# Sixty-four columns of ones in place of one in a kernel's column sums

## The reference, cut to what matters

```
def rms_norm(x, g):
    xf = x.astype(jnp.float32)
    y = xf * lax.rsqrt(jnp.mean(xf * xf, axis=-1, keepdims=True) + EPS)
    return (y * g.astype(jnp.float32)).astype(x.dtype)

def l2_norm(x):
    xf = x.astype(jnp.float32)
    return (xf * lax.rsqrt(jnp.sum(xf * xf, axis=-1, keepdims=True) + EPS)).astype(x.dtype)
...
    q = jnp.repeat(l2_norm(q), rep, axis=2) * DN_HEAD_DIM ** -0.5      # delta rule: 12 heads
    k = jnp.repeat(l2_norm(k), rep, axis=2)                            # 12 heads
...
    o = rms_norm(o.astype(p.dtype), out_g)                             # 24 heads of the mixer's output
...
    q = rms_norm(xq.reshape(B, S, XA_HEADS, XA_DIM), qn_g)             # cross-attention: 4 heads
    k = rms_norm(kv[..., :XA_WIDTH].reshape(B, -1, XA_HEADS, XA_DIM), kn_g)
```

## Time and profile before

| | us |
|---|---|
| median of 3 runs | 3015.46 |
| lowest and highest run | 3014.51, 3021.64 |
| profiled execution, its own time | 3011.83 |
| its span, first to last instruction | 3010.0 |
| PE busy / PEld busy | 2836.4 (94%) / 2672.0 (89%) |
| DVE busy / ACT busy / POOL busy | 1903.9 (63%) / 1411.2 (47%) / 386.0 (13%) |
| TensorE's mean granted clock | 0.973 of full speed |

### The profile page before, as it was taken

How to read it: one execution, slowest core, us unless ns; L and a number is a source line. 1 busy time by engine, 2 the same in 40 slices (tenths; PEclk the granted TensorE clock), 3 DMA queues, 4 the chain that set the end, 5 groups by cost and what they waited for, 6 DMA issues and landing times.

```text
span 3010.0 us, 46274 instructions
## 1 busy us (share of the span) xinstructions
PE 2836.4 (94%) x19298; PEld 2672.0 (89%) x19298; DVE 1903.9 (63%) x2814; ACT 1411.2 (47%) x2387; POOL 386.0 (13%) x360
## 2 busy tenths in 40 slices
PE   6999989889889999999989999998999999999997
PEld 6999989888888998999979999997888899987785
DVE  5546648533323544655456865776888888878786
ACT  5346543555654433444344204343555555555454
POOL 0000010211111000003100002221122211112320
PEclk9999989999999999999999999999999999999998
DMA  4443444422223554444434458998999988899894
GB/s 185 169 154 140 169 131 167 154 77 94 85 94 112 198 186 166 167 169 162 154 114 169 156 204 322 374 357 312 366 361 371 366 319 322 321 350 349 319 350 147
DMA packets 109680, 668.46 MB, mean 222 GB/s; under 512 B 25777, under 2 KB 26313, under 8 KB 31553
## 3 DMA queue, kind: packets, MB, share of 16 engines
q1 hardware_dynamic: 83808, 496.08, 45.2%
q0 software_dynamic: 24512, 164.97, 15.0%
q10 hardware_dynamic: 1152, 4.47, 0.4%
HBM read 651.54 MB, written 13.30 MB: 221 GB/s over the span
## 4 chain that ended last, share of the span: by engine, by line
PE 72%; DVE 12%; DMA 8%; ACT 7%; issue 2%; POOL 0%; SPq 0%; DVEq 0%; ACTq 0%
PE PS L1027 71%; DMA raw<-in_pv 4%; DVE WL L1641 4%; DVE m L1632 3%; DMA m<-in_pv,keep 3%; ACT m L2322 2%; ACT WH L2337 2%; ACT L2322 1%; DVE m L1841 1%; DVE m L2162 1%; DMA raw<-in_w_kv 1%; DVE m L1838 0%; PE PS L1030 0%; ACT m L2323 0%; DVE m L1660 0%
## 5 line engine op out<-in xcount | busy, mean ns | idle before, releaser
L1641 DVE TENSOR_TENSOR WL<-raw,WH 128x1024 fp32r<-128x1024 f32 x804 | 985.5, 1234 | 650.6 <-ACT WH L2337 649.6
L2337 ACT CAST WH<-raw 128x1024 fp32r<-128x1024 f32 x804 | 837.5, 1046 | 551.5 <-PE PS L1027 390.2
L1027 PE MATMUL PS<-m_4096r,WH 128*128 128x256 f32 x5184 | 997.3, 293 | 29.9 <-DVE m L1632 14.7
L1027 PEld LDWEIGHTS PS<-m_4096r,WH 128*128 128x128 f32 x5184 | 827.8, 196 | 53.2 <-DVE m L1632 16.1
L1027 PE MATMUL PS<-m_4096r,WL 128*128 128x256 f32 x2592 | 743.6, 287 | 0.0
L1027 PE MATMUL PS<-m_8192r,WH 128*128 128x256 f32 (+1 forms) x2560 | 559.7, 312 | 17.5 <-issue 11.1
L1027 PE MATMUL PS<-WH,m_896r 128*128 128x512 f32 x1536 | 523.1, 393 | 28.2 <-DVE m_896r L2255 27.9
L1027 PEld LDWEIGHTS PS<-m_4096r,WL 128*128 128x128 f32 x2592 | 507.6, 196 | 0.0
L1027 PEld LDWEIGHTS PS<-m_8192r,WH 128*128 128x128 f32 x2560 | 397.6, 193 | 20.3 <-issue 11.7
L1027 PE MATMUL PS<-m_8192r,WL 128*128 128x192 f32 (+1 forms) x1792 | 404.3, 272 | 0.0
L1027 PE MATMUL PS<-WL,m_896r 128*128 128x512 f32 x1024 | 400.8, 391 | 0.0
(11 more groups left out here) (234 smaller groups left out, 1857.7 us busy)
## 6 DMA issues: line engine op xcount, KB each, us to landing
raw<-in_pu SPq DMA_DIRECT2D x128, 1024.0 KB, 6.8
raw<-in_pv SPq DMA_DIRECT2D x128, 1024.0 KB, 8.0
raw<-in_w_qkv SPq DMA_DIRECT2D x48, 1024.0 KB, 4.8
raw<-in_w_o SPq DMA_DIRECT2D x48, 1024.0 KB, 4.8
raw<-in_w SPq DMA_DIRECT2D x40, 1024.0 KB, 4.8
raw<-in_w_z SPq DMA_DIRECT2D x32, 1024.0 KB, 4.8
raw<-in_w_kv SPq DMA_DIRECT2D x16, 1024.0 KB, 4.8
raw<-in_w_q SPq DMA_DIRECT2D x16, 1024.0 KB, 4.8
```

What stands on the lines that cost most here:

```text
L1027: return e.matmul(o, l, x, start=start, stop=stop)
L1641: tt(WL[:, k, :], raw[:, n % NRAW, h * 1024:h * 1024 + 1024], WH[:, k, :].bitcast(F), ALU.subtract).then_inc(S["lo"], 1)
L2337: e.copy(WH[:, k, :], raw[:, n % NRAW, h * 1024:h * 1024 + 1024]).then_inc(S["hi"], 1)
```

## The change

Every column sum now takes the first 64 columns of the tile of ones, so each gives 64 equal columns. The first of them stands where the one column stood; the other 63 stand to its right. Sums are issued in rising order of their column, so the next sum writes over what the last left to the right of its own column, and the columns that are read hold what they held before. In `hn_sum` the two matmuls of one sum write the same 64 columns, the second adding. Up to column 70 (`hn_sum`), 110 (`rn_sum`) and 66 (`dn_yss`) of the bank is written in place of 7, 47 and 3. No instruction is added or removed, no wait, no transfer and no order is changed.

```
+            def add_up(bank, c, x, start=True, stop=True):
+
+                return mm(PS[:, bank, c:c + 64], x, C("ones")[:, 0:64], start, stop)
...
-                            m = mm(PS[:, 2, 2 * h + t:2 * h + t + 1], tile(SQ, 2 * h + i)[:, tok(t)], C("ones")[:, 0:1],
-                                   i == 0, i == 1)
+                            m = add_up(2, 2 * h + t, tile(SQ, 2 * h + i)[:, tok(t)], i == 0, i == 1)
...
-                    m = mm(PS[:, 2, 2 * i + t:2 * i + t + 1], x[:, tok(t)], C("ones")[:, 0:1], True, True)
+                    m = add_up(2, 2 * i + t, x[:, tok(t)])
...
-                    m = mm(PS[:, bA, i:i + 1], blk(dn(g, "kb"), i), C("ones")[:, 0:1], True, True)
+                    m = add_up(bA, i, blk(dn(g, "kb"), i))
```

## The result

| | before | after |
|---|---|---|
| median, lowest to highest | 3018.38 us, 3014.51 to 3021.64 (5 runs) | 2995.59 us, 2993.34 to 3002.26 (5 runs) |
| profiled execution, its own time | 3011.83 us | 2993.34 us |
| its span | 3010.0 us | 2991.5 us |
| mean granted clock | 0.973 | 0.978 |

The ratio is 0.9929 with a 95% interval of 0.9914 to 0.9944: the change makes the kernel faster, as forecast, by 22.8 us between the medians. The forecast was a gain of 12.0 us, to 3003.5 us, with a range from 2998 to 3012. The measured time lies 2.4 us under the range. The two profiled executions lie 18.5 us apart.

What follows compares the result with a forecast made beforehand. TensorE was taken to bound the kernel on most of the way. 12.4 us back from the clock less 0.4 us latency gives 12.0 us off 3015.5, so 3003.5 us; range 2998 to 3012, chance 0.60.

Steps and rivals of the forecast that it cites:

- That the wider passes cost nothing: On TensorE, the 256 column-sum passes: 64 columns hide behind the next pass's weight load, 0 us; at most 13.6 us.
- That the clock holds in the padded blocks: TensorE's granted clock stays at 1.00 throughout all six `hn_sum` and `rn_sum` blocks, where 27.30 us had been at 0.50.
- The comparison with wide passes and pauses: From 29.48 to 36.30 us, 256-column passes kept 1.00 with TensorE busy 3.65 of 6.82 us; the padded block moves more.
- Rival B: No change (3015.9 us): the clock falls in the padded blocks too, only the latency of 0.4 us is paid; chance 0.10.
- The 12.4 us from the low stretches: Five half-clock stretches at `hn_sum` and `rn_sum`: 4.0 us back from column sums, 8.4 us from mostly weight passes.
- That the shift reaches the end unchanged: Behind 401.61 us ACT and DVE begin earlier by the same amount, so the whole gain reaches the end.
- Latency, 0.4 us: At 15 group ends ACT waits some 25 ns longer for the last matmul: 0.4 us added, between 0 and 0.8.
- `dn_yss`, 0: Padding these sums might save the low stretch at 940.84 us, 1.5 us; taken as 0 because the pause stays.
- A: Only part arrives (3009.5 us): where low stretches begin is chance, the changed kernel may fall elsewhere; 6 us back; chance 0.17.
- D: More (3000 us): timed runs lose 3.6 us more to the same stretches, or the 940.84 us stretch goes; chance 0.10.
- The Trainium skill's rule read as busy time: The clock follows how busy TensorE is, so the drops at busy one-column blocks have another cause and padding gives nothing.
- the last one of the sum: Whole kernel: the 12.0 us gain is taken from the three timed runs' median, 3015.5 us, giving 3003.5 us.

Runs made afterwards that it cites:

- second profile: The kernel before, unchanged, profiled and timed again in a later job: 3001.74 us median, ratio to the kernel before 0.998.
- fourfold sums: Every matmul of `rn_sum` issued four times over, against the kernel before: 3062.11 us with one column, 3036.99 us with 64 columns in `rn_sum` only.
- first and third: The kernel before, unchanged: profiled execution of 3011.83 us at first, and profiled and timed again in a later job, 3008.99 us, ratio 1.0005.

## Why the prediction was right and wrong

- **That the wider passes cost nothing**: right. 0.108 to 0.110 us a pass with 64 columns, against the 0.109 and 0.106 of the rows on either side; 128 columns cost nothing either.
- **That the clock holds in the padded blocks**: right in all four profiles of the changed kernel. The comparison with wide passes and pauses in the earlier trace rows led to the right answer. Rival B is excluded. The comparison rested on one stretch with wide passes, so that 64 columns would do was a well-founded guess and no more; 32 didn't do every time.
- **The 12.4 us from the low stretches**: right in size. The first pair of profiles shows 12.8 us at pass 2800, the mean of all profiles 11.0, since the kernel before doesn't lose the clock at every block in every execution. Two small terms were missed. The pause behind the queries' block is followed by a low stretch of its own, 6.83 us in the first profile before and 3.41 after, so 1.3 us more came back there (passes 1400 to 1600 take 33.0 us before and 28.6 after, 4.4 in place of the 3.1 of the block itself). That isn't shown to be the change's work: the kernel before has no such stretch at all in its second profile (27.2 us for the same passes), and of the five variants with one column in `hn_sum` three have 3.41 us too (at 231.40 us with 64 columns in `rn_sum` only) and the two with fourfold sums none. In the other direction, TensorE now reaches `iv_turn` before DVE has its gains ready and waits 0.54 us, the new wait of this change.
- **That the shift reaches the end unchanged**: supported, within the scatter. Behind pass 2800 the means of both kernels differ by 1.4 us.
- **Latency, 0.4 us; `dn_yss`, 0**: too small to be seen here.
- **Rivals A and D**: A's premise is right, as the second profile of the kernel before shows, but its fear that the changed kernel falls low elsewhere isn't borne out: outside the six blocks and in front of pass 2800 it spends 13.7 to 17.1 us at 0.50, the kernel before 13.7 to 20.5. D asked that the timed runs lose 3.6 us more to the same stretches; no run shows that, and the measured 2995.6 us lies under D's 3000 as well.
- **The Trainium skill's rule read as busy time** ("TensorE: Matmul & The Clock Gate", "Part 1: The HAM clock gate"): this case's runs disagree with that reading. Two stretches of the same 441 instructions, both 100% busy, ran at 0.56 and 1.00.
- **The step that failed** is the last one of the sum and the range built on it: "On their scale: 3015.5 - 12.0 = 3003.5 us". The gain was sized rightly; what was mis-sized is the 3015.5 that it was taken from, the median of three runs. In the three later jobs the kernel before ran 101 times, between 2991 and 3023 us, with a median of 3006.6. From there 12.0 us less are 2994.6, and the medians of the changed kernel are 2995.6 in the first comparison and 2995.2, 2993.8 and 2997.7 in the later ones (single runs between 2986 and 3004). So the changed kernel came out at its usual level, and the starting point was some 9 us above the usual level of the kernel before. The prediction had only 5.5 us below its forecast, and allowed for the runs' own scatter by one-sided mishaps (3.6 us in rival D).
- **Why the first comparison gave 22.8 us** and not 12.0: 2.9 of the 10.8 us more come from two further runs, which raised the median of the kernel before from 3015.46 to 3018.38. The later comparisons give 7 to 13 us between medians, so the rest didn't come again. The 5.7 us in the first pair of profiles are within what stages behind pass 2800 do by themselves: over kernels that do the same there they take from 2573.4 to 2595.3 us, the late gather above being one example. But all five timed runs of the kernel before lie at 3014.5 us or above, where only 12 of its 101 later runs lie. Neither a profile nor the granted clock of these five is on record, so whether chance or something of that chip put them there stays open.

## What to carry to other kernels

Look for stretches where TensorE is fully busy and the clock falls right behind: long rows of matmuls with very few moving columns. Where each pass carries its own weight load of 128 columns, as here, up to 128 moving columns were free (0.108 to 0.112 us a pass with 1, 32, 64 and 128), so widen the moving operand, or break the row up with wide passes. This gives back only what falls behind such rows, here 27.3 of 161.1 us at half clock; the stretches behind real pauses stay. And before giving a range for a change of half a per cent, look at how far runs of one kernel lie apart; compare the stage that the edit touches pass by pass, where 11 us were seen, rather than totals, and take the starting level from more than three runs.

## What the runs showed of the hardware that was not expected

- The same code loses the clock behind a given block in one execution and keeps it in another: the queries' block at 1.00 in the second profile of the kernel before, at 0.50 in the first and third. The keys' block too kept it once, in the kernel with fourfold one-column sums, where it began at 105.18 in place of 104.00; in the kernel beside it, where it began at 104.74, the clock fell:

```profile
105.18:112.00 6.82, 6.82 (x62) 6.82 (x61) 1.72 (x3) 1.48 (x3) 0.00 (x0) 1.00 0.17 67
```

- A fall costs more than its row: with fourfold sums the four rows of 96 one-column passes took 16.8 to 20.3 us from their first pass to the next instruction, where rows with 64 columns took 10.6. That is 29.3 of the 34.3 us; the other 5.0 were lost by the weight passes between and behind the rows.
- With the cause removed, the first 386.2 us repeated to 0.15 us in four executions, three of them on three different chips, while the remaining 2586 us scattered by 7.5.
